# One hybrid mLSTM and GLA decoder layer: the recurrence products of the GLA heads from rounded halves instead of unrounded operands

## What is computed

```python
def step(S, inp):                        # per chunk, per head
    qc, kc, vc, lc = inp
    b = jnp.cumsum(lc, axis=2)
    decay = jnp.exp(jnp.where(mask, b[:, :, :, None, :] - b[:, :, None, :, :], -jnp.inf))
    A = jnp.einsum('bhtd,bhsd,bhtsd->bhts', qc, kc, decay)
    o = jnp.einsum('bhts,bhsv->bhtv', A, vc) + jnp.einsum('bhtd,bhdv->bhtv', qc * jnp.exp(b), S)
    bL = b[:, :, -1, :]
    S_new = jnp.exp(bL)[..., None] * S + jnp.einsum('bhsd,bhsv->bhdv', kc * jnp.exp(bL[:, :, None, :] - b), vc)
    return S_new, o
```

## Time and profile before

| | |
|---|---|
| median of 3 runs | 1853.26 us (1850.15, 1853.26, 1853.49) |
| the profiled execution, its own time | 1850.89 us |
| its span | 1849.0 us |
| granted PE clock | 9 tenths or more in every slice |
| PE, PEld busy | 98%, 94% |
| DVE, ACT, POOL busy | 60%, 38%, 41% |
| windows B of heads 0 to 2 | about 237 to 341, 473 to 577, 709 to 813 us |
| window L | about 935 to 1009 us |

### The profile page before, as it was taken

The page is one execution under the profiler, slowest core; times in us unless marked ns, Lnnn a source line. Parts: engine busy times, 40 slices in busy tenths (PEclk is TensorE's granted clock), DMA queues, the critical chain, the costliest instruction groups (busy, mean ns, idle before and its releaser), DMA issues.

```text
span 1849.0 us, 36320 instructions
## 1 busy us (share of the span) xinstructions
PE 1815.6 (98%) x14583; PEld 1743.6 (94%) x14583; DVE 1104.6 (60%) x1930; ACT 711.8 (38%) x1477; POOL 751.6 (41%) x655
## 2 busy tenths in 40 slices
PE   8999999999999999999999999999999999999998
PEld 5899999999999999999989999989999999999998
DVE  6852744526454364543575688885666667566656
ACT  5544434344333443434435544223223222322327
POOL 4331432423333233332344774244345444544545
PEclk9999999999999999999999999999999999999999
DMA  9332232322223222232243641111112111211212
GB/s 324 113 94 58 79 91 73 121 58 78 86 70 119 64 83 81 70 112 64 83 140 104 216 129 51 42 47 52 41 47 69 32 60 48 60 33 47 69 47 94
DMA packets 182638, 154.80 MB, mean 84 GB/s; under 512 B 10324, under 2 KB 163092, under 8 KB 181960
## 3 DMA queue, kind: packets, MB, share of 16 engines
q1 hardware_dynamic: 182170, 152.27, 27.2%
q10 hardware_dynamic: 302, 0.22, 0.0%
HBM read 130.96 MB, written 21.50 MB: 82 GB/s over the span
## 4 chain that ended last, share of the span: by engine, by line
PE 84%; DVE 7%; issue 3%; POOL 3%; ACT 2%; DMA 1%; SPq 1%; ACTq 0%; DVEq 0%; POOLq 0%
PE bank L1056 27%; PE bank L2426 20%; PE bank L2395 12%; PE bank L1078 9%; PE bank L2293 3%; PE bank L1222 2%; PE bank L2260 1%; PE bank L1288 1%; PE bank L1247 1%; PE bank L1245 1%; POOL mix L1601 1%; PE bank L1250 1%; PE bank L1203 1%; PE bank L1277 1%; PE bank L1269 1%
## 5 line engine op out<-in xcount | busy, mean ns | idle before, releaser
L1056 PE MATMUL bank<-h_hi,w_by_parity 128*128 128x320 f32 (+2 forms) x2304 | 452.5, 329 | 1.5 <-POOL w_by_parity L1530 1.5
L1530 POOL TENSOR_TENSOR w_by_parity<-w_raw,w_by_parity 128x512 fp32r<-128x512 f32 x128 | 186.8, 1460 | 551.3 <-ACT w_by_parity L1304 551.3
L1056 PEld LDWEIGHTS bank<-h_hi,w_by_parity 128*128 128x128 f32 x2304 | 378.7, 188 | 17.6 <-issue 11.2
L1056 PE MATMUL bank<-h_lo,w_by_parity 128*128 128x384 f32 (+2 forms) x1152 | 232.9, 324 | 0.0
L2725 POOL TENSOR_TENSOR f_by_parity<-w_raw,f_by_parity 128x512 fp32r<-128x512 f32 x107 | 145.2, 1362 | 195.8 <-ACT f_by_parity L2490 195.8
L2725 POOL TENSOR_TENSOR w_by_parity<-w_raw,w_by_parity 128x512 fp32r<-128x512 f32 x107 | 144.2, 1353 | 149.4 <-ACT w_by_parity L2490 149.0
L1056 PEld LDWEIGHTS bank<-h_lo,w_by_parity 128*128 128x128 f32 x1152 | 194.2, 188 | 0.0
L3074 DVE SCALAR_TENSOR_TENSOR x_t<-bank,ada,x_t 128x352 f32<-128x352 f32 (+1 forms) x288 | 155.9, 568 | 56.0 <-PE bank L2395 38.5
L1078 PE MATMUL bank<-w_by_parity,h_hi 128*128 128x256 f32 x1024 | 170.1, 281 | 1.0 <-POOL w_by_parity L1530 1.0
L2395 PE MATMUL bank<-act_hi,f_by_parity 128*128 128x352 f32 x528 | 155.1, 325 | 1.5 <-POOL act_lo L2759 1.1
L2395 PE MATMUL bank<-act_hi,w_by_parity 128*128 128x352 f32 x528 | 154.1, 323 | 1.7 <-DVE ffn_temps L2859 1.6
(11 more groups left out here) (534 smaller groups left out, 3678.7 us busy)
## 6 DMA issues: line engine op xcount, KB each, us to landing
w_raw<-in_w_in SPq DMA_DIRECT2D x128, 256.0 KB, 3.0
w_ada_tile<-in_w_ada SPq DMA_DIRECT2D x32, 512.0 KB, 4.0
w_raw<-in_w_out SPq DMA_DIRECT2D x48, 256.0 KB, 2.9
w_raw<-in_w_ffn_gate SPq DMA_DIRECT2D x44, 256.0 KB, 3.0
w_raw<-in_w_ffn_up SPq DMA_DIRECT2D x44, 256.0 KB, 3.0
w_raw<-in_w_ffn_down SPq DMA_DIRECT2D x44, 256.0 KB, 3.0
w_ada_ring<-in_w_ada SPq DMA_DIRECT2D x10, 512.0 KB, 9.4
x_scratch<-x_turned_rows SPq DMA_DIRECT2D x1, 4224.0 KB, 16.7
```

Source lines behind the costliest of these rows:

```text
L1056: last = pe.matmul(g.ps[b][:, 0:n], slice_k(x[:, s], k), y[:, 4 * h + k, c0:c0 + n], start=(h == 0 and k == 0 and m == 0), stop=(h == 1 an ...
L1530: pool.tensor_tensor(lo, by_parity(raw[:, r]), hi.bitcast(F32), ALU.subtract).then_inc(s_lo, 1)
```

## The change

Four things are done to the GLA recurrence.

1. The three unrounded products of a chunk become three rounded products each, the code of the mLSTM chunk widened to both mixers (L1245, L1247 and L1250 are gone).
2. New stages make the halves. `recurrence_split`: ACT rounds scores and queries (four copies of 512 columns), DVE subtracts (two of 1024). `keys_split`: two copies, one subtraction. `values_split`: four copies on ACT, four subtractions on POOL, in windows B only once the convolution of the next head's keys is through (`s_silu`), since their buffer is the convolution's. After each state update ACT rounds the state and DVE subtracts.
3. In windows B the chunks move from behind pieces 31 to 38 to behind pieces 33 to 40, and `sample_out`, the samples and `norm` by one or two pieces. `gate_r0` moves from 33 to 32, and the load of the next head's decay row waits for chunk 7.
4. In window L `values_split` stands behind piece 4, the other splits behind 12, and the chunks, which stood behind 13, 13, 14, 15, 15, 16, 16, 17, stand in pairs behind 14, 15, 16 and 17.

```diff
     "B": [...
-          ("level7", 26), ("taps_k", 26), ("ada_load2", 26), ("masked", 30), ("keys", 30), ("ada2", 30), ("silu_k", 31),
-          ("chunk0", 31), ("ada_load3", 31), ("chunk1", 32), ("chunk2", 33), ("gate_r0", 33), ("decay_load", 33), ("chunk3", 34),
...
+          ("level7", 26), ("taps_k", 26), ("ada_load2", 26), ("recurrence_split", 27), ("masked", 30), ("keys", 30), ("ada2", 30),
+          ("silu_k", 31), ("keys_split", 31), ("values_split", 31), ("ada_load3", 31), ("ada3", 39),
+          ("chunk0", 33), ("chunk1", 34), ("chunk2", 35), ("chunk3", 36), ("chunk4", 37), ("chunk5", 38), ("chunk6", 39), ("chunk7", 40),
...
     "L": [...
+          ("level4", 4), ("values_split", 4), ("level5_k", 6), ("ada0", 6), ("level5", 7), ("gate_r0", 7),
...
@@ the chunk on PE, now for both mixers
+                    elif name in CHAIN and w != "S":
                         def three(bank, x, y, first, final):
                             for m, (p, r) in enumerate(((0, 0), (0, 1), (1, 0))):
+                                ins = pe.matmul(bank[:, 0:wide_], x[p][:, c * P:(c + 1) * P], y[r], start=(first and m == 0), stop=(final and m == 2))
                             return ins
+                        if isB(w):
+                            values, keys, queries = (values_hi_of(w, c), values_lo_of(c)[:, 0, :]), KD2B, QD2B
+                            pe.wait_ge(s_vlo, vlo_of_b(i, c))
+                            if c == 0:
+                                pe.wait_ge(s_rlo, rlo_of_b(i, "keys"))
...
+                        full(three(use(n), keys, values, True, True))
...
                         if c:
+                            pe.wait_ge(s_rlo, (rlo_of_b if isB(w) else rlo_of)(i, "state", c - 1))
@@ ACT
+                    elif name == "recurrence_split" and isB(w):
+                        act.wait_ge(s_qd, two(w, i) + 1)
+                        for to, x in ((scores_hi, AT), (queries_hi_b, QD)):
+                            for b in range(2):
+                                last = act.activation(to[:, 512 * b:512 * b + 512], x[:, 512 * b:512 * b + 512], ACT.Copy)
+                            last.then_inc(s_rhi, 1)
...
+                    elif name == "values_split" and isB(w):
+                        if w == "B":
+                            act.wait_ge(s_silu, i * 2 + 4)
+                        else:
+                            wait_use(act, "A", i, USE["A"]["turn1"] + 2)
+                        for c in range(0, NC, 2):
+                            act.activation(values_hi_of(w, c, 2).rearrange("p (c d) -> p c d", d=DV), v[:, c:c + 2, 0:DV], ACT.Copy).then_inc(s_rhi, 1)
...
+                        if w == "L" and c < NC - 1:
+                            wait_read_use(act, w, i, n)
+                            act.activation(state_of(w, c)[0], SS[:, c % 2, 0:DV], ACT.Copy).then_inc(s_rhi, 1)
@@ POOL
+                    elif name == "values_split" and isB(w):
+                        for c in range(0, NC, 2):
+                            pool.wait_ge(s_rhi, hi_of_b(w, i, "values", c))
+                            pool.tensor_tensor(values_lo_of(c, 2), V[1][:, c:c + 2, 0:DV],
+                                               values_hi_of(w, c, 2).rearrange("p (c d) -> p c d", d=DV).bitcast(F32), ALU.subtract).then_inc(s_vlo, 1)
@@ DVE, behind the state update
+                        if w in "BL" and c < NC - 1:
+                            dve.wait_ge(s_rhi, hi_of_b(w, i, "state", c))
+                            dve.tensor_tensor(state_of(w, c)[1], SS[:, c % 2, 0:DV], state_of(w, c)[0].bitcast(F32), ALU.subtract).then_inc(s_rlo, 1)
```

More of the change, by code:

```diff
@@ L790, in mixer_phase, with state_of, values_hi_of, values_lo_of @@
         AT2, KD2, QD2 = (scores_hi, scores_lo), (keys_hi, keys_lo), (queries_hi, queries_lo)
+        KD2B, QD2B = (keys_hi_b, keys_lo), (queries_hi_b, queries_lo)
+        def state_of(w, c):
+            at, x = (2 * (c % 2) * DV, xal) if w == "L" else (3 * P, state_halves_b)
+            return x[:, at:at + DV], x[:, at + DV:at + 2 * DV]
+        def values_hi_of(w, c, n=1):
+            if w == "L":
+                return g.values_hi_l[:, c * DV:(c + n) * DV]
+            return g.values_hi_b[c // 4][:, c % 4 * DV:(c % 4 + n) * DV]
+        def values_lo_of(c, n=1):
+            return values_lo_b[:, c * VE:(c + n) * VE].rearrange("p (c d) -> p c d", d=VE)[:, :, 0:DV]
         s_w = g.s_w
@@ L1016, in window @@
                         else:
-                            sp.wait_ge(s_qd, two(w, i) + 1)
+                            wait_use(sp, w, i, USE[w]["chunk7"] + 1)
                         nxt = 0 if w == "S" else i + 1
@@ L1231, in window @@
                         if c:
[L1232 removed]
                             at = 2 * ((c - 1) % 2)
[L1234 to L1250 removed]
+                            pe.wait_ge(s_rlo, (rlo_of_b if isB(w) else rlo_of)(i, "state", c - 1))
+                            last = three(bank, queries, state_of(w, c - 1) if isB(w) else (SS2[:, at, :], SS2[:, at + 1, :]), False, True)
                         full(last)
@@ L1460, in window @@
                         act.activation(KD[:, SEQ:SEQ + P], RB(n + 2)[:, 0:P], ACT.Copy).then_inc(free(n + 2), 1)
+                    elif name == "recurrence_split" and isB(w):
[4 more added lines that the diff above has]
+                            last.then_inc(s_rhi, 1)
+                    elif name == "keys_split":
+                        wait_read(act, w, i, "keys")
+                        for b in range(2):
+                            last = act.activation(keys_hi_b[:, 512 * b:512 * b + 512], KD[:, 512 * b:512 * b + 512], ACT.Copy)
+                        last.then_inc(s_rhi, 1)
+                    elif name == "values_split" and isB(w):
+                        if w == "B":
+                            act.wait_ge(s_silu, i * 2 + 4)
+                        else:
+                            wait_use(act, "A", i, USE["A"]["turn1"] + 2)
+                        for c in range(0, NC, 2):
+                            act.activation(values_hi_of(w, c, 2).rearrange("p (c d) -> p c d", d=DV), v[:, c:c + 2, 0:DV], ACT.Copy).then_inc(s_rhi, 1)
                     elif name == "values_split":
@@ L1488, in window @@
                         act.activation(dst, RB(u)[:, 0:vw], ACT.Copy).then_inc(s_hc, 1)
+                        if w == "B" and c < NC - 1:
+                            wait_read_use(act, w, i, n)
+                            act.activation(state_of(w, c)[0], SS[:, c % 2, 0:DV], ACT.Copy).then_inc(s_rhi, 1)
                         act.wait_ge(s_hc, two(w, i, NT) + (c + 1))
@@ L1707, in window @@
                         dve.tensor_tensor(QD[:, :], QD[:, :], q[:, :], ALU.mult).then_inc(s_qd, 1)
+                    elif name == "recurrence_split" and isB(w):
+                        for what, x, split in (("scores", AT, (scores_hi, scores_lo)), ("queries", QD, QD2B)):
+                            dve.wait_ge(s_rhi, hi_of_b(w, i, what))
+                            dve.tensor_tensor(split[1][:, 0:SEQ], x[:, 0:SEQ], split[0][:, 0:SEQ].bitcast(F32), ALU.subtract).then_inc(s_rlo, 1)
+                    elif name == "keys_split":
+                        dve.wait_ge(s_rhi, hi_of_b(w, i, "keys"))
+                        dve.tensor_tensor(keys_lo[:, 0:SEQ], KD[:, 0:SEQ], keys_hi_b[:, 0:SEQ].bitcast(F32), ALU.subtract).then_inc(s_rlo, 1)
                     elif name == "recurrence_split":
@@ L3188, in build @@
             g.va = va
+        with nc.sbuf_tensor("values_hi_last", [P, NC * DV], F32R) as last_values_hi:
+            g.values_hi_l = last_values_hi
         fx = sb("f_by_parity", [P, 2, ODD], F32R)
```

60 lines of the change are left out of this document (28 added, 32 removed), and 12 rows, old and new, of the table AT_SLOT.

## The result

| | before | changed |
|---|---|---|
| median of 11 runs each, on one chip | 1852.27 us (1849.81 to 1854.26) | 1857.23 us (1853.99 to 1862.39) |
| the profiled execution, its own time | 1850.89 us | 1857.23 us |
| its span | 1849.0 us | 1854.9 us |

The ratio is 1.0029, with a 95% interval of 1.0019 to 1.0038: **slower by 5.0 us**, where 3.2 were forecast and called no measurable change. The time lies in the range; the sign falls on the side of "slower by over 0.2%".

The account below looks back on a forecast made before the run. PE, 98% busy, was taken to bound the kernel, plus its few waits. Terms -6.7 + 3.5 + 1.3 + 2.1 + 3.0 = +3.2 on 1850.89 gave 1854.1, at the runs' median 1856.5 us; range 1848.3 to 1860.5.

Parts of the forecast that it names:

- no measurable change: Call on the whole kernel: +3.2 us lies within 0.2%, 3.7 us, close to the upper edge; chance of within 0.43.
- products: On PE, three rounded products replace each unrounded one, 0.073 us saved each, 92 products: -6.7 us, 5.0 in B, 1.7 in L.
- level chain in L: In L, POOL's four subtractions ahead of `k_decayed` make it end at 956.4, not 952.88, delaying level 5: +3.5 us.
- chunk 0 in L: In L, PE waits at chunk 0 for ACT's six copies and DVE's last remainder: +1.3 us.
- pairs in L: In L's chunk pairs, PE waits for state remainders, the gate delaying the second pair: +2.1 us, ends 1.1 and 3.0.
- B windows: Waits of 0.5 at chunk 0, 0.3 for the first state remainder, 0.2 at the end: 1.0 a window, +3.0 us in three.
- B's first remainder: In B, the first state remainder is late by 0 to 0.75 us as ACT and DVE leave splits and gate; taken as 0.3.
- DVE and POOL in each other's way: Rival: in B and L, DVE and POOL instructions hold each other up for a whole instruction; +6.6, 1859.9 us; chance 0.30.
- Its own sign: Deciding sign: first state remainder ends after PE's sixth group behind piece 34, some 3.2 us behind chunk 0's start.
- my forecast: Main case, whole kernel: both rivals hold partly; +3.2 us, 1856.5 us, spanning 1853 to 1859; chance 0.45.
- samples and `norm` late: At a B window's end, samples and `norm` stand one or two pieces later: 0 to 0.5 us, taken as 0.2.
- Only PE counts: Rival: POOL's 4.41 us gap in L hides the subtractions, level 5 starts on time; 1848.3 to 1849.6 us; chance 0.25.

Follow-up runs that it names:

- e9: As e7, but the last chunk of windows B stands behind piece 41 instead of in a pair behind 40; 1846.70 us, ratio 0.9970 to the kernel before.
- e6: e2 with ACT's four value roundings and POOL's four subtractions added behind piece 4 of L, results unread; 1854.93 us, ratio 1.0016 to the kernel before.
- e10: The changed kernel run again with nothing changed; 1858.84 us, ratio 1.0042 to the kernel before.
- e3: The changed kernel with rounded products in window L only, B windows as in the kernel before; 1857.45 us, ratio 1.0027 to the kernel before.
- e4: The changed kernel, but in windows B DVE's `gate_r0` stands behind piece 30, ahead of the SiLU; 1858.04 us, ratio 1.0030 to the kernel before.
- e8: As e5, with L's pairs behind 15 to 18 and the gate ahead of the first pair; 1855.57 us, ratio 1.0019 to the kernel before.
- e11: As e8, but DVE does the gate between `q_decayed` and the first remainder; 1854.64 us, ratio 1.0017 to the kernel before.
- e1: The changed kernel, but in L ACT rounds the values behind piece 10 and POOL subtracts behind level 7; 1855.17 us, ratio 1.0015 to the kernel before.
- e2: The changed kernel with rounded products in windows B only, L as in the kernel before; 1852.37 us, ratio 1.0000 to the kernel before.
- e5: As e1, but ACT rounds L's values one piece earlier, behind piece 9; 1853.38 us, ratio 1.0010 to the kernel before.
- e7: e2 with B's chunks one piece later, the last two paired behind 40, `ada3` beside `sample_out`, `gate0` one later; 1848.59 us, ratio 0.9982 to the kernel before.

## Why the prediction was right, and where it was not

The forecast and what the traces show, in us against the kernel before:

| term | forecast | measured |
|---|---|---|
| products | -6.7 | 23 a B window -1.77, L -1.7: -7.0; e9 shows 4.9 of B's 5.3 by themselves |
| level chain in L | +3.5 | +3.48; alone in e6 3.0 to 3.6 |
| chunk 0 in L | +1.3 | +1.57 |
| pairs in L | +2.1 | +2.29 |
| B windows | +3.0 | +5.2 (1.75 each); by the landmarks +5.0 |
| sum | +3.2 | +5.6; by the runs +5.0 |

- **The mechanism was right in each term but the last part of B's**: chain, chunk 0, pairs, B's chunk 0, B's first remainder. The price per product, the 3.5 of the chain and its landing place on POOL came out to a tenth.
- **The call did not come out.** "No measurable change" stood for less than 3.7 us, and 5.0 is more. That the time itself was met to 0.7 us (1856.5 against 1857.2) is in part luck: the base of 1853.3, from three runs, was 1.0 above the 1852.3 of eleven. By the difference, 3.2 against 5.0, the miss is 1.8.
- **The term that failed is B windows.** I took 0.5 + 0.3 + 0.2 a window. Chunk 0 cost 0.64, the first state remainder 0.46, the end 0.65. The rival "DVE and POOL in each other's way" had 0.65, 0.75 and 0.5: right for the first, and nearer than mine in sum, 1.9 against 1.0. Its own sign came true too, in all three B windows: the first state remainder ends 3.55 us behind the start of chunk 0 (541.34 + 1.30 - 539.09), later than the 3.2 it asked for. In L it was too high (3.8, 1.9 and 3.0 for what cost 3.48, 1.57 and 2.29). So this is a result between the two cases, DVE and POOL in each other's way in B and my forecast in L. The last was called samples and `norm` late; in fact those were on time, and it is five changes from one kind of product to another, 0.1 each, which no row of mine had priced. Nor had I priced the slow product behind each wait.
- **Lost elsewhere, and in no term:** 0.3 us in each of two A windows that follow a B window (the drift goes from 0.42 at 341 to 0.72 at 383 us, and from 0.68 at 817 to 0.95 at 855), in the changed kernel, e10 and e9 alike. The change leaves these windows' tables alone; the cause was not looked for.
- **"Only PE counts"** needed `k_decayed` by 953.15 on the old scale. It ended at 957.31 - 0.97 = 956.34, where I had 956.4.
- **Not foreseen: the clock.** Nothing in the sum had it. In the changed kernel's two profiled executions it is absorbed; where it falls behind level 6 (e3, e4, e8, e11) it adds 1.5. The lower clock is not confined to the profiled executions. Over all runs, those with the 3.2 us wait (the changed kernel, e10, e3, e4, e6; 47 runs) have a mean granted clock of 0.9963, e1, e2, e5, e7 and e9 (53 runs) 0.9975, and the kernel before (the 83 runs beside e1 to e11) 0.9972. Only the mean is known of a run, not where in it the clock was lost. The changed kernel's times also spread more, 8.4 us from lowest to highest against 4.4 before, and its two longest runs have its lowest clocks (1862.39 us at 0.993, 1860.97 at 0.994); that all of the spread is the clock's doing was not shown.
- The Trainium skill's rule that a DVE instruction with two SBUF inputs and a GpSimd one that reads SBUF exclude each other for a whole instruction (SBUF — State Buffer, Who interferes with whom) fits every long row above: 2.25 for 1.26, 1.94 for 1.36, 1.57 for 0.74, 1.44 for 0.43. As a forecast of the total, +6.6, the rival overshot 5.0 by 1.6, about as much as mine fell short.
- The Trainium skill (FP8 and Floating Point Precision, TensorE Precision Notes) has true float32 in four passes; three for four, 0.108 a product, would by this estimate save 2.5 a B window. e9 measured 1.7. The rows were right.

What stays open: why e10's ratio is above the first one, what the A windows lose, the shares of rounding and subtraction in the chain, and what decides on which side of level 6 the clock falls.

## What to carry to other kernels

Cheaper products pay only where their operands come early enough: the changed kernel loses 5.0 us, and e9, with the chunks one piece later in B and the window without slack left as it was, wins 5.2. Price a new elementwise stage by what is queued behind it on its engine (POOL's four subtractions stood ahead of the one `k_decayed` that everything waits for), and look at POOL before moving a DVE instruction into DVE's idle time, and the reverse. A wait costs more than its length: count the slow product behind it, and on a kernel that keeps PE full, the clock.

## What the runs showed of the hardware that I had not expected

- Behind the 3.2 us wait for level 5 the granted clock fell to the low level in all five traces that have it (the changed kernel twice, e3, e4, e6), for 3 to 4 us, in e6 for nearly 7. PE's products took 1.5 us longer by it each time, 2.3 in e6. In eight traces whose longest wait there is 2.0 (before, e1, e2, e5, e7, e8, e9, e11) it stayed up in six and fell in two, e8 and e11.
- Even shorter waits come with a fall in some traces and not in others. Around 90 us, in code that the change leaves alone, PE waits 1.3 to 1.5 and then 1.0 us in all thirteen traces; the clock fell behind that in six (e1, e2, e4, e6, e8, e9) and stayed up in seven. The kernel before, then e1, PE and by stretch:

```profile
89.95 0.74 PE L1078 MATMUL bank<-w_by_parity,h_hi 128*128 128x256 f32 x4 [1.01 <-POOL w_by_parity L1530]
90.00:95.00 5.00, 5.00 (x51) 4.83 (x52) 4.89 (x18) 0.70 (x2) 2.27 (x1) 1.00 0.41 99
```

```profile
90.92 1.23 PE L1105 MATMUL bank<-w_by_parity,h_hi 128*128 128x256 f32 x4 [1.01 <-POOL w_by_parity L1572]
90.00:95.00 5.00, 4.08 (x30) 3.94 (x30) 3.51 (x8) 1.67 (x3) 3.15 (x2) 0.66 0.44 112
```

The Trainium skill (TensorE: Matmul & The Clock Gate, Part 1: The HAM clock gate) says of a kernel's start that the number of slow products differs from run to run. Here it is whether a slow stretch comes at all that differs, between traces with the same code and nearly the same waits at that place.

- The first product behind a wait takes 0.19 to 0.22 us to the next start instead of 0.12, and a change between a chunk's products and those on `w_ada_tile` or `sample_state` costs about 0.1.
- At 243 us, ahead of the first chunk of a B window, the traces already stand -0.2 to +3.2 us from that of the kernel before, with nothing changed in that stretch. The six with the slow stretch at 90 us stand at 2.1 to 3.2 (e1 2.35, e4 3.21), the others at -0.2 to 1.4 (e10 -0.23, the changed kernel 0.58). Another comes at 1235 to 1250 us in seven traces, that of the kernel before among them. Only drifts inside a window say anything about it.
